# The first head of the two even attentions packed in two halves, the second head packed after the first exps, and the exp table loaded at the end of the stage before

## The reference, cut to what matters

```python
def forgetting_attention(q, k, v, log_f):            # "fox": own keys per head
    ...
        s = jnp.einsum('bqhd,bkhd->bhqk', qb, k, preferred_element_type=F32) * scale
        s = s + (cq[..., :, None] - cum[..., None, :])
        s = jnp.where(kpos[None, :] <= qpos[:, None], s, -jnp.inf)
        p = jax.nn.softmax(s, axis=-1)
        return jnp.einsum('bhqk,bkhd->bqhd', p.astype(v.dtype), v)

def dsa_attention(q, k, v, qi, ki, wi, topk):        # "dsa": one key head, 256 selected keys
    ...
        _, sel = lax.top_k(iscore, topk)
    ...
        s = jnp.einsum('bqhd,bqkd->bhqk', qb, k_sel, preferred_element_type=F32) * scale
        s = jnp.where(valid[:, None], s, -jnp.inf)
        p = jax.nn.softmax(s, axis=-1)
        return jnp.einsum('bhqk,bqkd->bqhd', p.astype(v.dtype), v_sel)
```

## Time and profile before

| | us |
|---|---|
| median of 3 runs | 2482.63 |
| lowest and highest run | 2479.14, 2482.97 |
| profiled execution, its own time | 2488.2 |
| its span | 2486.3 |
| fox stage in it, from 354.35 to 518.99 | 164.64 |
| dsa stage in it, from 518.99 to 658.5 | 139.5 |

### The profile page before, as it was taken

One profiled execution on the slowest core, in us unless ns is written; L12 is line 12 of the kernel. 1 busy time (PEld: TensorE's weight loads), 2 busy tenths in 40 slices (PEclk: granted clock), 3 DMA queues, 4 the chain that ended last, 5 costly groups with the idle time before them and its releaser, 6 DMA issues. The chain is left out here.

```text
span 2486.3 us, 31702 instructions
## 1 busy us (share of the span) xinstructions
PE 2319.7 (93%) x11379; PEld 1942.3 (78%) x11379; DVE 1757.3 (71%) x2652; ACT 1199.0 (48%) x1961; POOL 852.5 (34%) x656
## 2 busy tenths in 40 slices
PE   6899979989799999999999969899889999999996
PEld 4678768889777788888888757698767888888885
DVE  4676677865544788888789844556568888887995
ACT  4457777666442434434444633355433444444453
POOL 2112113311011687787200001032257778770000
PEclk9999989999999999999999989989989999999998
DMA  4101001000142122222473521211122222227535
GB/s 144 35 26 51 26 18 35 19 1 1 67 137 81 64 77 79 91 85 77 170 245 95 168 94 43 63 57 50 62 77 76 77 93 85 77 77 242 182 123 157
DMA packets 189063, 212.85 MB, mean 86 GB/s; under 512 B 14788, under 2 KB 135972, under 8 KB 188908
## 3 DMA queue, kind: packets, MB, share of 16 engines
q1 hardware_dynamic: 183344, 193.30, 24.7%
q10 hardware_dynamic: 5564, 17.52, 1.8%
HBM read 170.83 MB, written 39.94 MB: 85 GB/s over the span
## 5 line engine op out<-in xcount | busy, mean ns | idle before, releaser
L126 PE MATMUL trunk_ps<-l_bhi,l_ahi 128*128 128x512 f32 x528 | 205.6, 389 | 2.0 <-DVE l_blo L2733 2.0
L126 PE MATMUL trunk_ps<-l_bhi,l_alo 128*128 128x512 f32 x528 | 205.4, 389 | 0.0
L126 PE MATMUL trunk_ps<-l_blo,l_ahi 128*128 128x512 f32 x528 | 205.4, 389 | 0.0
L126 PE MATMUL trunk_ps<-l_t_hi,l_s_hi 128*128 128x512 f32 x456 | 177.5, 389 | 0.0
L126 PE MATMUL trunk_ps<-l_t_hi,l_s_lo 128*128 128x512 f32 x456 | 177.4, 389 | 0.0
L126 PE MATMUL trunk_ps<-l_t_lo,l_s_hi 128*128 128x512 f32 x456 | 177.4, 389 | 0.0
L2395 POOL TENSOR_TENSOR l_s_lo<-l_raw,l_s_hi 128x512 fp32r<-128x512 f32 x90 | 160.2, 1788 | 42.4 <-ACT l_s_hi L2303 42.4
L2184 ACT ACTIVATE l_ahi<-l_a 128x512 fp32r<-128x512 f32 x132 | 83.3, 631 | 176.9 <-PE trunk_ps L126 166.3
L2395 POOL TENSOR_TENSOR l_s_lo<-l_w_sum,l_s_hi 128x512 fp32r<-128x512 f32 x76 | 119.5, 1575 | 48.6 <-ACT l_s_hi L2303 48.6
L204 POOL TENSOR_TENSOR wring_w_lo<-wring_raw,wring_w_hi 128x1024 fp32r<-128x1024 f32 x22 | 52.7, 2396 | 236.1 <-ACT wring_w_hi L200 236.1
L2730 DVE TENSOR_TENSOR l_alo<-l_a,l_ahi 128x512 fp32r<-128x512 f32 x132 | 91.1, 690 | 45.5 <-ACT l_ahi L2184 45.5
(11 more groups left out here) (469 smaller groups left out, 6820.8 us busy)
## 6 DMA issues: line engine op xcount, KB each, us to landing
l_draw<-in_ffn_w_out SPq DMA_DIRECT2D x154, 256.0 KB, 2.7
l_raw<-in_ffn_w_in SPq DMA_DIRECT2D x48, 512.0 KB, 4.6
gated_dram<-l_gate_out SPq DMA_DIRECT2D x44, 512.0 KB, 2.6
l_a<-gated_dram SPq DMA_DIRECT2D x88, 256.0 KB, 4.0
wring_raw<-in_even_w_in SPq DMA_DIRECT2D x20, 512.0 KB, 3.9
l_raw_g<-in_ffn_w_in SPq DMA_DIRECT2D x20, 512.0 KB, 3.8
l_raw_v<-in_ffn_w_in SPq DMA_DIRECT2D x20, 512.0 KB, 4.9
l_wt<-in_ffn_w_out SPq DMA_DIRECT2D x22, 256.0 KB, 4.3
```

Of the source, the lines that this page charges most:

```text
L126: mm = pe.matmul(o, w, m, start=a, stop=z, skip_group_check=onto)
```

## The change

In both attention stages head 0 is packed in two halves of 512 columns, by first_head_hi on ACT and first_head_lo on DVE, with one semaphore step for each operation, so that DVE starts after the first copies and not after the last. PE starts the scores when the first half is packed (first_lo at 3) and waits for the second half (first_lo at 6) ahead of the scores of block 4, which is part 4. DVE packs the first half, runs bias_max of parts 0 and 1, and packs the second half then. ACT copies both halves (in fox with the two mask copies between them) ahead of the exps, as before. The high part of head 1 moves on ACT: it was packed right after that of head 0, and now stands at j=0 behind the exps of blocks 0 to 3 and ahead of the copy of part 0. POOL's packing of head 1 waits for it, and no longer for DVE's packing of head 0. At the front's end ACT runs an exp of 128 x 1 elements, for the sake of the table load that goes with it.

```diff
@@ even_front_stage, ACT, end of the stage
                 sc.wait_ge(fv_taken, TB)
+                sc.activation(prod[0][:, 0:1], g.const[:, K_ONE:K_ONE + 1], ACT.Exp)
@@ causal_stage
         def pack_head_lo(engine, h):
             x, r, k = heads[h]
-            engine.wait_ge(hi_packed, h + 1)
-            if h >= 1:
-                engine.wait_ge(lo_packed, h)
+            engine.wait_ge(hi_packed, h)
+            if h >= 2:
+                engine.wait_ge(lo_packed, h - 1)
...
+        def first_head(half):
+            x, r, k = heads[0]
+            own, other = halves(r)
+            c = slice(HALF * half, HALF * half + HALF)
+            if keys is None:
+                return c, k[own, c], (own, other), own, x[own, c], own, other
+            return c, keys[0][:, c], halves(0), key_rows[0], x[own, c], own, other
+
+        def first_head_hi(act, half):
+            c, key, rows, _, query, own, _ = first_head(half)
+            for to in rows:
+                act.activation(k_hi[0][to, c], key, ACT.Copy).then_inc(first_hi, 1)
+            act.activation(q[0][own, c], query, ACT.Copy).then_inc(first_hi, 1)
+
+        def first_head_lo(dve, half):
+            c, key, rows, hi_rows, query, own, other = first_head(half)
+            for i, to in enumerate(rows):
+                dve.wait_ge(first_hi, 3 * half + 1 + rows.index(hi_rows))
+                dve.tensor_tensor(k_lo[0][to, c], key, k_hi[0][hi_rows, c].bitcast(F32), ALU.subtract).then_inc(first_lo, 1)
+            dve.wait_ge(first_hi, 3 * half + 3)
+            dve.tensor_tensor(q[0][other, c], query, q[0][own, c].bitcast(F32), ALU.subtract).then_inc(first_lo, 1)
@@ PE, scores(j)
-                    if j == first[TB * h]:
-                        pe.wait_ge(lo_packed, h + 1)
-                    if j == 0 and keys is not None:
-                        pe.wait_ge(key_lo, 2 * nkeys)
+                    if j == first[TB * h] and h:
+                        pe.wait_ge(lo_packed, h)
+                    if j in (0, first[TB // 2]):
+                        pe.wait_ge(first_lo, 3 if j == 0 else 6)
@@ ACT
-                for i in range(0 if keys is None else nkeys):
-                    for r in range(2):
-                        act.activation(k_hi[i][HD * r:HD * r + HD, :], keys[i], ACT.Copy).then_inc(key_hi, 1)
-                pack_head_hi(act, 0)
+                first_head_hi(act, 0)
                 if forget:
...
-                pack_head_hi(act, 1)
+                first_head_hi(act, 1)
                 done = 0
                 for j in range(NPARTS):
...
                     while done < N and first[done] <= j + EXP_AHEAD:
                         exp(done)
                         done += 1
+                    if j == 0:
+                        pack_head_hi(act, 1)
                     if not by_dve[j]:
                         copy(j)
@@ DVE
-                for i in range(0 if keys is None else nkeys):
-                    dve.wait_ge(key_hi, 2 * i + 2)
-                    for r in range(2):
-                        dve.tensor_tensor(k_lo[i][HD * r:HD * r + HD, :], keys[i], k_hi[i][key_rows[i], :].bitcast(F32), ALU.subtract).then_inc(key_lo, 1)
-                pack_head_lo(dve, 0)
+                first_head_lo(dve, 0)
                 groups = chore = 0
                 for j in range(NPARTS + AHEAD + BEHIND + 1):
                     if j < NPARTS:
                         bias_max(j)
+                    if j == 1:
+                        first_head_lo(dve, 1)
```

More of the change, by code:

```diff
@@ L1524, in causal_stage @@
         copied_act, copied_dve, summed, rs_ready, O_taken = (st.sem(x) for x in ("copied_act", "copied_dve", "summed", "rs_ready", "O_taken"))
-        hi_packed, lo_packed, key_hi, key_lo, k_lo_packed = (st.sem(x) for x in ("hi_packed", "lo_packed", "key_hi", "key_lo", "k_lo_packed"))
+        hi_packed, lo_packed, k_lo_packed = st.sem("hi_packed"), st.sem("lo_packed"), st.sem("k_lo_packed")
+        first_hi, first_lo = st.sem("first_hi"), st.sem("first_lo")
         if forget:
@@ L1559, in pack_head_lo @@
                                          ALU.subtract).then_inc(k_lo_packed, 1)
-                    engine.wait_ge(k_lo_packed, 2 * h + i + 1)
+                    engine.wait_ge(k_lo_packed, 2 * h + i - 1)
             pack_lo(engine, q[h % 2], x, r).then_inc(lo_packed, 1)
+        def first_head(half):
[17 more added lines that the diff above has]
+            dve.tensor_tensor(q[0][other, c], query, q[0][own, c].bitcast(F32), ALU.subtract).then_inc(first_lo, 1)
         packing = {first[TB * h] - AHEAD + 1: h + 1 for h in range(1, HEADS - 1)}
@@ L1583, in _ @@
                     pack_head_lo(pool, h)
-                pool.wait_ge(lo_packed, HEADS)
+                pool.wait_ge(lo_packed, HEADS - 1)
             @block.tensor
```

## The result

The change made the kernel slower: median 2488.04 us (2481.67 to 2494.68) against 2480.74 us (2475.48 to 2486.45) of the kernel before on the same chip, ratio 1.0025 with a 95% interval of 1.0016 to 1.0034. The medians stand 7.3 us apart; the ratio, which this document goes by, makes it 6.2 us, between 4 and 8.4. The profiled execution took 2489.45 us, its span 2487.2 us.

What follows compares the result with a forecast made beforehand. PE, busy 93% of the span, bounds the kernel; its two stage-start waits allow at most 12.9 us. Front +0.8, fox -0.15, dsa -0.35 and clock 0 give +0.3 on the median of 2482.63: 2482.9 us, range 2478.5 to 2487.5.

Steps and rivals of the forecast that it cites:

- The front: At the front's end, the exp and its table load delay the barrier by +0.8 us, bounds +0.5 to +1.0.
- The head start and its return in fox (a, b): Fox start: PE 4.15 us earlier; DVE's second half, then ACT's head 1 packing, cut the gain to 0.1 us.
- POOL at part 12 (c): Fox, head 1: POOL packs later, so PE gets part 12 at 21.1 instead of 20.5, 0.6 us late.
- what is left at the packing of head 2: Fox, head 2's packing: -0.15 us remains, all orders the old ones from there; bounds -2.1 to +1.5.
- The rival of the low clock: Fox's first head: waits hold PE at 1.2 GHz until t = 26, losing up to 6 us, 2488.9; chance 0.05.
- Dsa: Dsa stage: PE starts at 3.4 instead of 5.94, part 0's values at 10.45 instead of 10.79; -0.35 us, bounds -1.0 to +1.0.
- The clock of 0.50: Stage starts: 1.2 GHz ends by t = 9.0 in fox, 6.4 to 9.5 in dsa, covered by PE's wait for ACT; cost 0.

Runs made afterwards that it cites:

- e3: The changed kernel with DVE's selection pieces in fox begun three parts later; ratio to the kernel before 1.0013.
- e2: The changed kernel without the exp at the front's end; ratio to the kernel before 1.0017.
- e4: The kernel before with only head 1's packing moved behind the exps of blocks 0 to 3, no halves, no front exp; ratio to the kernel before 1.0030.
- e1: The changed kernel with head 1's high part packed by ACT ahead of the first exps, as before the change; ratio to the kernel before 1.0006.
- e5: The changed kernel with head 1 packed ahead of the exps and no front exp, so only the halves; ratio to the kernel before 1.0000.
- e6: e5 with ACT's three packing copies for each of fox's heads 2 to 7 spread over three parts; ratio to the kernel before 0.9982.
- e8: e6 with unused matmuls on constants: one in fox and two in dsa at the start, one more ahead of part 4's scores; ratio to before 0.9957.
- e7: e6 with the halves in fox alone, dsa packing as before the change; ratio to the kernel before 0.9963.
- e9: The kernel before with only the packing of heads 2 to 7 spread over three parts, no halves; ratio to the kernel before 0.9963.
- e10: e7 with unused matmuls on constants at the stage starts, one in fox and four in dsa; median 2469.01 us, ratio to the kernel before 0.9952.

## Why the prediction was right in most steps and wrong in the sum

It said 2482.9, up to 2487.5, and no difference that can be told; the change cost 0.25%, 6 us, just beyond both. (The range as it was added up, -2.3 - 2 and +3.5 + 2, would be 2478.3 to 2488.1 and was stated narrower at both ends; 2488.04 lies at the upper edge of it.) The terms of fox and of dsa were mis-sized, and one rival weighed too little.

- **The front**: predicted +0.8, measured +0.45. The load (1.28 us) and the exp (0.17, predicted 0.23) came as expected. The barrier follows ACT by 0.27 us, and I had taken DVE's 0.58. The Trainium skill's drain of 1.38 us per load (ScalarE: Activation LUTs, What ACT_TABLE_LOAD costs) is not seen: the exp begins 0.02 us behind the load.
- **The head start and its return in fox (a, b)**: PE's first matmul at t = 2.72 (predicted 2.85), the copy of part 0 at 13.70 (13.6), the values of part 0 at 14.03 (13.95). The queue's order ate the gain, as said.
- **POOL at part 12 (c)**: 21.09, predicted 21.1.
- **The term that failed**: what is left at the packing of head 2, -0.15. It was +1.4 (part 24 at 40.17 against 38.75, without a fall). I priced POOL's move to t = 13.75 to 21.04 only by who waits for POOL. It also runs beside other DVE work than before, and one DVE step is held up by 2.1 us, to 2.31; ACT's exp of block 7 goes late by as much, then head 2's packing, and PE's wait is 1.57 instead of 0.78. e3 takes the step out of POOL's way and the 1.4 us are gone. The price could have been read ahead of the change, from collisions of the kernel before (see e3). The Trainium skill (SBUF — State Buffer, Who interferes with whom) has the rule: DVE and GpSimd share a pair of ports as "an exclusive lock", the later one blocks for the whole instruction, and tensor_scalar is in its list of operations that can do so. The trace agrees: 2.31 us, from 0.07 us behind POOL's start to POOL's end, and 0.23 us elsewhere.
- **The rival of the low clock**, chance 0.05, price 6 us: it is part of what happened, at another place. I looked for a clock that does not come back from the stage's start. In the kernel after it came back and fell again behind the longer wait, at a price of 4.85 us, in two of three profiles with this order (after and e2, not the second of after). In e4 it was the first place as well. The Trainium skill (TensorE: Matmul & The Clock Gate, A second HAM failure mode) tells of a clock that goes back and forth where PE stands idle for short times and often between groups of matmuls. Here the falls stand behind single waits of 1.6 us and more. I had set the rival aside for the mean clock of the earlier trace rows, which held two such falls already.
- **Dsa**: predicted -0.35. Against the two profiles of before (139.51 and 140.83) the two of after (140.39 and 140.30) give +0.2 on average, with part 12 at 17.9 and 17.8 against 17.0 and 18.3. PE's first matmul came at 3.49 (3.4). The clock of 0.50 lasts until t = 12, longer than the 6.4 to 9.5 I gave it, and I had priced it at nothing because PE would wait for ACT. It doesn't: ACT's copy of part 0 starts at 10.41 (10.15) and is done at 10.7, and PE, busy with slow matmuls since 7.4, comes to the values of part 0 only at 11.31 (10.45). In fox the clock came back at 12.5 and 12.8 and not at 9.0, and there PE's wait for ACT until 14.03 did cover it.

By the timed kernels: moving head 1's packing 4.7 us (after against e1), the exp in the front 1.5 us (e1 against e5, 0.45 by the traces), the halves 0.0 (e5). These are differences along one chain of ratios, so that they add up to the 6.2 us is no evidence, and only the first is clear of the intervals. e4 shows the same cause from the other side: the packing moved in the kernel before costs 0.30%, 5 to 10 us. By the traces, fox is 165.6 us on average over the three profiles with the order of the kernel after and 163.0 over the two of before, +2.6; with +0.2 in dsa and +0.45 in the front that is 3.2 of the 6.2 us. The rest no profile here shows. The runs of the kernel after lie 13 us apart, and one fall of the clock more or less is 5 us.

What stays open: how often the clock falls in head 1 of the changed kernel, for which three profiles are too few; why the same waits, within 0.01 us, are followed by a fall in one execution and not in the next; and how much of dsa's late part 12 (20 us in e1, e5, e6 and e8) is the collision's, which stands in all four, and how much the clock's, which is low until t = 14.3 to 15.3 in all four.

## What to carry to other kernels

A step moved to another time is priced twice: by who waits for it, and by what now runs beside it. For a long POOL operation list the DVE instructions in its new window, the tiny ones too, and what is queued behind each. Here one move of ACT's packing put POOL beside a DVE step in fox and took it away from one in dsa. And where PE is busy 93% of the time, look for its repeated waits of 1.5 to 2 us before its one long wait at the start: taking apart ACT's three copies for the next head brought 0.4%, while starting PE 4.3 us earlier brought nothing that could be measured.

## What the hardware showed that I had not expected

- A DVE operation on 128 x 6 elements took 2.31 us beside a POOL subtraction of 2.36 us, and 0.23 us otherwise; a DVE subtraction of 64 x 512 took 2.74 us beside one of 2.35 us, and 0.69 us otherwise (e1). DVE's row minima of up to 512 columns ran beside the same POOL work at their usual time.
- The granted clock fell in the middle of steady work, 1.9 us behind a wait of 1.57 us, for 10.2 us, and did not in another execution with the same wait of 1.58 us. Behind waits of 1.1 us or less in fox it never fell (five profiles with the spread packing).
- In dsa the clock came back at t = 9.0 to 12.0 with PE's start in one piece (before twice, e4, e7, e9), at 11.3 to 12.1 with a start in pieces and head 1 packed late (after twice, e2, e3), and at 14.3 to 15.3 in pieces with head 1 packed first (e1, e5, e6, e8). The first two ranges overlap. Four matmuls on constants in the wait had it back by t = 3.9 (e10).
- The barrier at the front's end passed 0.27 us behind ACT where ACT came last (after), and 0.58 us behind DVE where DVE did (before).
